# Attention over tiles of 128 neighbouring tokens, with score rows in four strips by residue

## The chip, the cores and the metric

The kernel runs on one core of one Trainium2 chip. The metric is the device time of one execution in microseconds. Before the change three runs gave a median of 2524.17 us (2521.6 to 2528.89).

## The reference

One inference step of a two-layer decoder, for a prompt of 512 tokens and 8 sample sequences of 8 tokens, 576 columns in all, model width 1024. Layer 0 mixes with a Mamba-2 SSD block, layer 1 with a dilated sliding-window attention; each is placed between two half-weighted SwiGLU feed-forward blocks. The change touches the attention of the prompt:

```
for g, (win, dil) in enumerate(((128, 1), (512, 4), (2048, 16))):     # 8 heads of 64 in each group
    idx = qi[:, None] - dil * j[None, :]            # j = 0 .. win // dil: keys by stride
    s = q . k[idx] - slope[g, h] * dil * j          # masked where idx < 0
    o[g], lse[g] = softmax(s) @ v[idx], logsumexp(s)
w = softmax(lse over the three groups);  out = sum_g w[g] * o[g]      # then @ w_o
```

Since the groups' outputs are weighted by their softmax denominators, one softmax over the keys of all three groups gives the same. For head h of each group the kernel therefore takes a single softmax over the keys of group 0 (the last 129 tokens), of group 1 (earlier tokens of the same residue modulo 4) and of group 2 (of the same residue modulo 16).

## The kernel before

The kernel runs as instruction streams written out by hand for each engine (SyncE starts DMAs, GpSimd, ScalarE, TensorE, VectorE), synchronized by counted semaphores. Each engine executes its stream in order. Activations stand feature-major, 576 tokens along the free axis.

Large products are made in three parts of split fp32 (`product`, L1441): high weights by high and by low activations, then low weights by high activations; a unit of 128 output features is 48 matmuls of 288 columns. ScalarE makes the high part of the weights (L895), GpSimd the low part (L743). ScalarE's `high_u` (L903) and VectorE's `low_u` (L2141) make the parts of the normalized input; for the attention (n == 4) both write the 512 prompt tokens permuted, residue t of 4 first, then a = token // 4, so that `qkv` holds tokens by residue. VectorE also makes a permuted copy of the reciprocal root (`rmp`, L2811).

`attention` has four turns (`turn(c, last)`), each with two heads of every group. The nine units of projections of turn 0 come first. In turns 0 to 2 the nine projection units of the next turn (`ahead(k)`) are interleaved with the attention of this one; the last turn has none. A turn has in order:

- 12 transposes of the values (L1977), copied out by ScalarE;
- for the tile t of 128 queries of residue t: `wide_scores` against all 512 keys of group 0 (L1962), one matmul a head, and `narrow_scores` against the 128 keys of the same residue in groups 1 and 2 (L1969), one a head and group;
- `softmax_in` on VectorE (L2850): three bias operations, slope times distance plus score, 512, 128 and 128 wide, a maximum over 768 and its negation; `exps` on ScalarE (L1332) with the sum; `normalize` on VectorE (L2866);
- 12 transposes of probabilities (L2021) in three groups of four, `probs_out` on ScalarE for each group (L1350, L1352);
- `values` (L2024): six blocks of 128 keys for each of two heads, L2033;
- `heads_out` (L1356) and `heads_low` (L2904), the high and low parts of the head outputs, written back in the permuted order;
- the sample's attention in steps between these (`sample_scores` L1991, `sample_step`), on a bank of its own; `sample_own` on VectorE stands ahead of `normalize(0)`;
- the output projection of the turn (L2110 to L2112), 48 matmuls.

In turns 0 to 2 the order on TensorE for a tile t is: projection, sample step, transposes group 0, wide scores of t + 1, transposes group 1, narrow scores of t + 1, transposes group 2, projection, sample step, values. In the last turn scores run two tiles ahead. An fp32 matmul stands in the trace as two records, each with a weight load, a transpose as one.

## Time and profile before

| | us |
|---|---|
| median of three runs | 2524.17 |
| the profiled execution | 2517.44 |
| its span | 2515.6 |
| TensorE busy | 2448.1 |
| VectorE busy | 1892.7 |
| ScalarE busy | 1421.6 |

The attention begins at about 1729 us of the span with the first projection; its turns begin at 1792.7, 1884.5, 1979.0 and 2073.4 us, and the last output projection starts at 2114.8. The profiled execution's own time is its span and what lies around it. TensorE's busy time counts modelled ends of pipelined matmuls, so the distance between the starts of neighbouring records says more on its pace than a record's length. "PEld" rows are its weight loads.

### The profile page before, as it was taken

The page shows a single profiled execution, that of the slowest core. Times are in us where ns is not written, and L with a number is a line of the kernel's source. Part 1 is how long each engine was busy: PE and PEld are TensorE (multiplying, and loading weights), DVE is VectorE, ACT ScalarE, POOL GpSimd, SP SyncE. Part 2 cuts the span into 40 slices and gives each one's busy share as a digit, 9 for nine tenths or more (in the row PEclk, how much of TensorE's full clock was granted, in tenths as well). Part 3 has the DMA queues.
Part 4 walks back from the last instruction along what each step waited for, and adds up shares of the span by engine and source line. Part 5 has one row for each costly group of instructions (what it writes and reads, how often), then busy time and mean ns, then how long its engine had stood idle before and what let it go on. Part 6 is the DMA issues. An engine that isn't in the chain of part 4 may idle for free.

```text
span 2515.6 us, 48796 instructions
## 1 busy us (share of the span) xinstructions
PE 2448.1 (97%) x18955; PEld 2372.2 (94%) x18955; DVE 1892.7 (75%) x3121; ACT 1421.6 (57%) x2417; POOL 742.5 (30%) x682
## 2 busy tenths in 40 slices
PE   8999999899999998999999999999999997999998
PEld 8999999799999988999999999999998996999998
DVE  8979767878888888979776978765345448987875
ACT  7757553445555556757566757554223236766663
POOL 2222233454444542222222222223322220222223
PEclk9999999899999998999999999999999999999999
DMA  7776743123333325767655777754433423777763
GB/s 204 168 163 168 168 114 101 44 95 103 103 103 103 98 77 151 169 163 168 158 131 139 169 169 161 170 128 149 145 109 123 138 91 86 163 169 166 164 156 91
DMA packets 107137, 341.92 MB, mean 136 GB/s; under 512 B 13824, under 2 KB 17536, under 8 KB 88512
## 3 DMA queue, kind: packets, MB, share of 16 engines
q1 hardware_dynamic: 53952, 242.78, 29.0%
q0 software_dynamic: 52992, 96.49, 22.8%
q8 instruction: 131, 2.15, 0.3%
q14 instruction: 62, 0.51, 0.1%
HBM read 223.44 MB, written 19.32 MB: 96 GB/s over the span
## 4 chain that ended last, share of the span: by engine, by line
PE 85%; DVE 7%; ACT 3%; issue 3%; DMA 2%; POOL 0%; DVEq 0%; SPq 0%; ACTq 0%; POOLq 0%
PE ps L1551 14%; PE ps L1557 14%; PE ps L1549 14%; PE ps L1451 7%; PE ps L1452 7%; PE ps L1457 7%; PE ps L1566 2%; PE ps L1567 2%; DMA sb_lw<-sb_rawf 2%; PE ps L1574 2%; PE ps L1866 1%; PE ps L1867 1%; PE ps L1868 1%; PE ps L1498 1%; PE ps L1490 1%
## 5 line engine op out<-in xcount | busy, mean ns | idle before, releaser
L1551 PE MATMUL ps<-sb_ual,sb_hw 128*128 128x288 f32 x2240 | 612.2, 295 | 0.0
L1549 PE MATMUL ps<-sb_uah,sb_hw 128*128 128x288 f32 x2240 | 608.1, 294 | 0.0
L760 POOL DMA_DIRECT2D sb_lw<-sb_rawf x336 | 289.8, 864 | 961.7 <-ACT sb_lw L930 939.3
L1551 PEld LDWEIGHTS ps<-sb_ual,sb_hw 128*128 128x128 f32 x2240 | 421.2, 188 | 0.0
L1549 PEld LDWEIGHTS ps<-sb_uah,sb_hw 128*128 128x128 f32 x2240 | 420.5, 188 | 0.0
L1557 PE MATMUL ps<-sb_uah,sb_lw 128*128 128x288 f32 x2240 | 384.1, 293 | 1.6 <-DMA sb_lw<-sb_rawf 1.0
L743 POOL TENSOR_TENSOR sb_wl<-sb_raw,sb_wh 128x1024 fp32r<-128x1024 f32 (+1 forms) x106 | 260.2, 2458 | 424.7 <-ACT sb_wh L895 408.7
L1451 PE MATMUL ps<-sb_uh,sb_wh 128*128 128x288 f32 x1360 | 377.4, 304 | 5.8 <-DVE sb_zs L2578 3.2
L1452 PE MATMUL ps<-sb_ul,sb_wh 128*128 128x288 f32 x1360 | 369.4, 298 | 0.0
L1557 PEld LDWEIGHTS ps<-sb_uah,sb_lw 128*128 128x128 f32 x2240 | 328.0, 188 | 3.2 <-DMA sb_lw<-sb_rawf 1.7
L1451 PEld LDWEIGHTS ps<-sb_uh,sb_wh 128*128 128x128 f32 x1360 | 258.2, 190 | 15.7 <-issue 7.0
L929 ACT CAST sb_hw<-sb_rawf 128x512 fp32r<-128x512 f32 x336 | 207.7, 618 | 92.1 <-PE ps L1557 81.6
L1452 PEld LDWEIGHTS ps<-sb_ul,sb_wh 128*128 128x128 f32 x1360 | 258.4, 190 | 0.4
L1549 PE MATMUL ps<-sb_hh,sb_hw 128*128 128x288 f32 x896 | 244.1, 294 | 3.9 <-DVE sb_x L2331 3.9
L1551 PE MATMUL ps<-sb_hl,sb_hw 128*128 128x288 f32 x896 | 243.9, 295 | 0.0
L895 ACT CAST sb_wh<-sb_raw 128x1024 fp32r<-128x1024 f32 (+1 forms) x106 | 111.5, 1052 | 182.7 <-PE ps L1457 126.4
L930 ACT ACTIVATE sb_lw<-sb_rawf 128x512 fp32r<-128x512 f32 x336 | 211.5, 629 | 0.0
L2204 DVE TENSOR_TENSOR sb_lw<-sb_tw,sb_hw 128x1024 fp32r<-128x1024 f32 x112 | 137.2, 1225 | 95.3 <-ACT sb_hw L964 90.6
L964 ACT CAST sb_hw<-sb_tw 128x1024 fp32r<-128x1024 f32 x112 | 117.8, 1052 | 136.5 <-PE ps L1557 136.5
L1457 PE MATMUL ps<-sb_uh,sb_wl 128*128 128x288 f32 x1360 | 194.1, 295 | 0.0
L1457 PEld LDWEIGHTS ps<-sb_uh,sb_wl 128*128 128x128 f32 x1360 | 185.0, 188 | 0.0
L1549 PEld LDWEIGHTS ps<-sb_hh,sb_hw 128*128 128x128 f32 x896 | 168.1, 188 | 5.7 <-issue 5.5
(346 smaller groups left out, 5197.2 us busy)
## 6 DMA issues: line engine op xcount, KB each, us to landing
sb_lw<-sb_rawf POOLq DMA_DIRECT2D x368, 256.0 KB, 3.8
sb_rawf<-w_ffn_in SPq DMA_DIRECT2D x87, 1024.0 KB, 5.3
sb_rawf<-w_ffn_so SPq DMA_DIRECT2D x32, 1024.0 KB, 5.6
sb_raw<-w_ssd SPq DMA_DIRECT2D x64, 512.0 KB, 3.6
sb_raw<-w_att SPq DMA_DIRECT2D x40, 512.0 KB, 3.6
sb_rawf<-w_ffn_out SPq DMA_DIRECT2D x32, 384.0 KB, 3.0
sb_h<-state SPq DMA_DIRECT2D x8, 1024.0 KB, 4.9
ssm_sample<-sb_h SPq DMA_DIRECT2D x8, 1024.0 KB, 4.7
```

Source lines behind the costliest of these rows:

```text
L743: pool.tensor_tensor(wl[parity][:, 0:width], raw[:, parity, 0:width], wh[parity][:, 0:width].bitcast(F32), ALU.subtract).then_inc(wl_done, 1)
L760: pool.dma_start(slot(lw, p), rawf[:, s % 2, i * BL:(i + 1) * BL], accum_op=ALU.add).then_inc(ld_in[i], 16)
L929: nc.scalar.copy(slot(hw, p), src).then_inc(hd_done, 1)
L930: nc.scalar.activation(slot(lw, p), src, ACT.Copy, scale=-1.0).then_inc(nd_done, 1)
L964: nc.scalar.copy(slot(hw, 7, 2), tw[:, 2 * BL:4 * BL]).then_inc(ht34_done, 1)
L1451: pe.matmul(ps[:, b, 0:n], w, rh[:, k, t0:t0 + n], start=first and k == 0, stop=False)
L1452: pe.matmul(ps[:, b, 0:n], w, rl[:, k, t0:t0 + n], start=False, stop=False)
L1457: ins = pe.matmul(ps[:, b, 0:n], w, rh[:, k, t0:t0 + n], start=False, stop=last and k == nk - 1)
L1549: pe.matmul(out, w[:, k * P:(k + 1) * P], high[k], start=begins and k == 0, stop=False, skip_group_check=True)
L1551: pe.matmul(out, w[:, k * P:(k + 1) * P], low[k], start=False, stop=False, skip_group_check=True)
L1557: ins = pe.matmul(out, v[:, k * P:(k + 1) * P], high[k], start=False, stop=k == 3, skip_group_check=True)
L2204: V.tensor_tensor(slot(lw, 7, 2), tw[:, 2 * BL:4 * BL], slot(hw, 7, 2).bitcast(F32), ALU.subtract).then_inc(lt34_done, 1)
```

## The change

The projections now write `qkv` in the tokens' own order. `high_u`, `low_u` and the reciprocal root lose their permuted forms. A tile t is the 128 neighbouring tokens 128 t to 128 t + 127; its score rows are arranged in four strips of 32 partitions, one for each residue q modulo 4. For each strip and head, near scores are one matmul with 32 stationary columns (the queries of residue q, 4 elements apart) against 128 (t = 0) or 256 contiguous keys of group 0; far scores, for groups 1 and 2, are one matmul against the 32 (t + 1) keys of that residue, 4 elements apart. A tile thus has 24 score matmuls in place of 6, and its keys are 192, 384, 448 or 512 wide in place of 768.

All scores of a head lie in one bank, so one bias operation covers them, with a table whose group 1 and 2 columns carry the ratio of the slopes. `pr` gets two buffers for tiles. The transposes (3 a head for t = 0, 4 otherwise, in place of 6; those of far keys are 32 (t + 1) columns wide) go back into the bank of the scores and are copied out once a head. `values` has 2 or 4 matmuls of near keys with 128 columns and 16 of far keys with 32 (t + 1) rows and 32 columns, in place of 12. The value transposes of groups 1 and 2 read their tiles 4 elements apart. On TensorE the transposes of a tile now stand together, both heads' scores follow the values two tiles ahead, and scores(0) and scores(1) stand at the head of every turn.

The diff, cut to what the prediction speaks of:

```diff
+KEYS = (192, 384, 448, 512)
...
-            pt = at("pt", [P, 2, 768])
-            pr = at("pr", [P, 2, 768])
-            d0 = at("d0", [P, CH, SEQ])
+            pt = at("pt", [P, 2, SEQ])
+            pr = at("pr", [P, 2, 2, SEQ])
+            dist = at("dist", [P, sum(KEYS)])
...
+        def of_residue(ap, r):
+            return ap.rearrange("p (b r) -> p r b", r=DIL)[:, r, :]
...
+        def by_residue(ap):
+            return ap.rearrange("p (b r) -> p r b", r=DIL)
+        def residue(ap):
+            return ap.rearrange("p (r b) -> p r b", r=DIL)
...
+        def near_keys(t):
+            return P * min(t + 1, 2)
...
+        def far_keys(t):
+            return 32 * (t + 1)
...
+        def score_bank(t, j):
+            return 4 + 2 * (t % 2) + j
...
+        def head_bank(t, last):
+            return t % 2 if last else 2
...
-                if n == 4:
-                    dst = uh[:, m, 0:SEQ].rearrange("p (t a) -> p t a", t=DIL)
-                    nc.scalar.activation(dst, perm(x[:, m, 0:SEQ]), ACT.Copy, scale=gains[:, n, one(m)])
-                    nc.scalar.activation(uh[:, m, SEQ:TOK], x[:, m, SEQ:TOK], ACT.Copy,
-                                         scale=gains[:, n, one(m)]).then_inc(uh_done, 1)
-                elif n != last_norm:
+                if n != last_norm:
                     nc.scalar.activation(uh[:, m, :], x[:, m, :], ACT.Copy, scale=gains[:, n, one(m)]).then_inc(uh_done, 1)
...
-                        nc.scalar.activation(pr[:, e % 2, :], pr[:, e % 2, :], ACT.Exp, bias=nmx[:, e:e + 1],
+                        t, j = e // 2, e % 2
+                        p = pr[:, t % 2, j, 0:KEYS[t]]
+                        nc.scalar.activation(p, p, ACT.Exp, bias=nmx[:, e:e + 1],
                                              accum_out=den[:, e:e + 1]).then_inc(exp_done, 1)
...
-                    def probs_out(t, i):
-                        act.wait_ge(pt_mm, c * 12 + (3 * t + i + 1))
-                        if t and i == 0:
+                    def probs_out(t, j):
+                        act.wait_ge(pt_mm, c * 8 + (2 * t + j + 1))
+                        if t and j == 0:
                             act.wait_ge(pv_mm, c * 4 + t)
...
+                        w = near_keys(t) + 2 * P
+                        nc.scalar.copy(pt[:, j, 0:w], ps[:, score_bank(t, j), 0:w]).then_inc(pt_done, 1)
...
                     def heads_out(t):
                         act.wait_ge(pv_mm, c * 4 + (t + 1))
-                        nc.scalar.copy(perm(oh[:, 0:SEQ])[:, t, :], ps[:, head_bank(last), 0:P]).then_inc(oh_done, 1)
+                        nc.scalar.copy(by_residue(oh[:, rows(t)]), residue(ps[:, head_bank(t, last), 0:P])).then_inc(oh_done, 1)
...
-                    def wide_scores(t):
-                        if t:
-                            pe.wait_ge(max_done, c * 8 + 2 * t)
+                    def scores(t):
+                        near, n = near_keys(t), far_keys(t)
+                        if t >= 2:
+                            pe.wait_ge(pt_done, c * 8 + (2 * (t - 2) + 2))
                         for j in range(2):
                             r = slice(HD * j, HD * j + HD)
-                            pe.matmul(ps[:, 4 + j, :], qkv[r, 0, rows(t)], qkv[r, 1, 0:SEQ], start=True, stop=True)
-                    def narrow_scores(t):
+                            for q in range(DIL):
+                                pe.matmul(ps[32 * q:32 * q + 32, score_bank(t, j), 0:near], of_residue(qkv[r, 0, rows(t)], q),
+                                          qkv[r, 1, (t + 1) * P - near:(t + 1) * P], start=True, stop=True)
                         for g in (1, 2):
-                            for j in range(2):
-                                r = slice(HD * j, HD * j + HD)
-                                ins = pe.matmul(ps[:, 6 + j, rows(g - 1)], qkv[r, 3 * g, rows(t)],
-                                                qkv[r, 3 * g + 1, rows(t)], start=True, stop=True)
+                            for q in range(DIL):
+                                for j in range(2):
+                                    r = slice(HD * j, HD * j + HD)
+                                    far = ps[32 * q:32 * q + 32, score_bank(t, j), near + (g - 1) * n:near + g * n]
+                                    keys = of_residue(qkv[r, 3 * g + 1, 0:DIL * n], q)
+                                    ins = pe.matmul(far, of_residue(qkv[r, 3 * g, rows(t)], q), keys, start=True, stop=True)
                         ins.then_inc(sc_mm, 1)
...
-                    for g in range(AG):
-                        for t in range(CH):
-                            ins = pe.transpose(ps[:, value_bank(g), rows(t)], qkv[:, 3 * g + 2, rows(t)], ident[:, :])
+                    for t in range(CH):
+                        ins = pe.transpose(ps[:, value_bank(0), rows(t)], qkv[:, 2, rows(t)], ident[:, :])
+                    ins.then_inc(vt_mm, 1)
+                    for g in (1, 2):
+                        for q in range(DIL):
+                            ins = pe.transpose(ps[:, value_bank(g), rows(q)], of_residue(qkv[:, 3 * g + 2, 0:SEQ], q), ident[:, :])
                         ins.then_inc(vt_mm, 1)
...
                     pe.wait_ge(ao_evac, c * 8 + 1)
-                    wide_scores(0)
-                    narrow_scores(0)
+                    scores(0)
+                    scores(1)
...
+                    def transposes(t, j):
+                        pe.wait_ge(norm_done, c * 8 + (2 * t + j + 1))
+                        near, n = near_keys(t), far_keys(t)
+                        for k in range(near // P):
+                            pe.transpose(ps[:, score_bank(t, j), rows(k)], pr[:, t % 2, j, rows(k)], ident[:, :])
+                        for g in (1, 2):
+                            probs = pr[:, t % 2, j, near + (g - 1) * n:near + g * n]
+                            ins = pe.transpose(ps[0:n, score_bank(t, j), rows(near // P + g - 1)], probs, ident[:, :])
+                        ins.then_inc(pt_mm, 1)
+                    def values(t):
+                        blocks, n = near_keys(t) // P, far_keys(t)
+                        pe.wait_ge(pt_done, c * 8 + (2 * t + 2))
...
+                            pe.wait_ge(ol_done, c * 4 + (t - 1 if last else t))
+                        for k in range(blocks):
                             for j in range(2):
                                 r = slice(HD * j, HD * j + HD)
-                                v = vt[:, max(0, k - 3), k if k < 4 else t, r]
-                                ins = pe.matmul(ps[r, head_bank(last), 0:P], v, pt[:, j, rows(k)], start=k == 0, stop=k == 5)
+                                pe.matmul(ps[r, head_bank(t, last), 0:P], vt[:, 0, t + 1 - blocks + k, r], pt[:, j, rows(k)],
+                                          start=k == 0, stop=False, skip_group_check=True)
+                        for g in (1, 2):
+                            for q in range(DIL):
+                                at = (blocks + g - 1) * P + 32 * q
+                                for j in range(2):
+                                    r = slice(HD * j, HD * j + HD)
+                                    ins = pe.matmul(ps[r, head_bank(t, last), 32 * q:32 * q + 32], vt[0:n, g, q, r],
+                                                    pt[0:n, j, at:at + 32], start=False, stop=g == 2, skip_group_check=True)
                         ins.then_inc(pv_mm, 1)
...
-                        wide_scores(1)
-                        narrow_scores(1)
                         for t in range(CH):
-                            for i in range(3):
-                                transposes(t, i)
+                            for j in range(2):
+                                transposes(t, j)
                             sample_step((0, 2, 4, 0)[t])
                             values(t)
                             if t < CH - 2:
-                                wide_scores(t + 2)
-                                narrow_scores(t + 2)
+                                scores(t + 2)
...
-                            transposes(t, 0)
-                            if t < CH - 1:
-                                wide_scores(t + 1)
-                            transposes(t, 1)
-                            if t < CH - 1:
-                                narrow_scores(t + 1)
-                            transposes(t, 2)
+                            for j in range(2):
+                                transposes(t, j)
                             pe.wait_ge(q_evac, c * 9 + (10 + 2 * t))
                             ahead(2 * t + 1)
                             sample_step(2 * t + 1)
                             values(t)
+                            if t < CH - 2:
+                                scores(t + 2)
...
                 g = gains[:, n, one(m)]
-                if n == 4:
-                    for v in ((lambda a: perm(a[:, m, 0:SEQ]), lambda a: a[:, m, 0:SEQ].rearrange("p (t a) -> p t a", t=DIL)),
-                              (lambda a: a[:, m, SEQ:TOK],) * 2):
-                        ins = V.scalar_tensor_tensor(v[1](ul), v[0](x), g, v[1](uh).bitcast(F32), ALU.mult, ALU.subtract)
-                    ins.then_inc(u_ready, 1)
-                else:
-                    V.scalar_tensor_tensor(ul[:, m, :], x[:, m, :], g, uh[:, m, :].bitcast(F32),
-                                           ALU.mult, ALU.subtract).then_inc(u_ready, 1)
+                V.scalar_tensor_tensor(ul[:, m, :], x[:, m, :], g, uh[:, m, :].bitcast(F32),
+                                       ALU.mult, ALU.subtract).then_inc(u_ready, 1)
...
-                dve.wait_ge(att_const, 80)
-                V.tensor_copy(rmp[:, 0:SEQ].rearrange("p (t a) -> p t a", t=DIL), perm(rms[:, 0:SEQ]))
-                step(V.tensor_copy(rmp[:, SEQ:TOK], rms[:, SEQ:TOK]))
+                dve.wait_ge(att_const, 64)
...
-                    d, src, r = two(dst), ps[:, b:b + 2, 0:HALF], two(rmp[:, :])
+                    d, src, r = two(dst), ps[:, b:b + 2, 0:HALF], two(rms[:, :])
...
-                        if t:
-                            dve.wait_ge(pt_mm, c * 12 + (3 * t - 1 + j))
-                        V.scalar_tensor_tensor(pr[:, j, 0:SEQ], d0[:, t, :], slp[:, one(c * 2 + j)], ps[:, 4 + j, :],
-                                               ALU.mult, ALU.add)
-                        for g in (1, 2):
-                            o = slice(SEQ + (g - 1) * P, SEQ + g * P)
-                            ins = V.scalar_tensor_tensor(pr[:, j, o], d12[:, g - 1, :], slp[:, one(c * 2 + (AH * g + j))],
-                                                         ps[:, 6 + j, rows(g - 1)], ALU.mult, ALU.add)
-                        step(ins)
-                        step(V.reduce_max(nmx[:, e:e + 1], pr[:, j, :], AX.X))
+                        if t >= 2:
+                            dve.wait_ge(pt_mm, c * 8 + (2 * (t - 2) + j + 1))
+                        p = pr[:, t % 2, j, 0:KEYS[t]]
+                        step(V.scalar_tensor_tensor(p, dist[:, sum(KEYS[:t]):sum(KEYS[:t + 1])], slp[:, one(c * 2 + j)],
+                                                    ps[:, score_bank(t, j), 0:KEYS[t]], ALU.mult, ALU.add))
+                        step(V.reduce_max(nmx[:, e:e + 1], p, AX.X))
...
-                        V.tensor_scalar(pr[:, e % 2, :], pr[:, e % 2, :], rcp[:, e:e + 1], None, ALU.mult).then_inc(norm_done, 1)
+                        p = pr[:, e // 2 % 2, e % 2, 0:KEYS[e // 2]]
+                        V.tensor_scalar(p, p, rcp[:, e:e + 1], None, ALU.mult).then_inc(norm_done, 1)
```

## Rows read from the trace of the kernel before

**Rows 1.** The page's busy times of the engines.

```profile
PE 2448.1 (97%) x18955; PEld 2372.2 (94%) x18955; DVE 1892.7 (75%) x3121; ACT 1421.6 (57%) x2417; POOL 742.5 (30%) x682
```

**Rows 2.** Busy time by window: start:end, length, then PE, PEld, DVE, ACT, POOL, clock, DMA.

```profile
1733.00:1792.70 59.70, 56.83 (x408) 56.03 (x408) 15.63 (x15) 10.76 (x11) 23.70 (x12) 0.97 0.51 181
1792.70:1884.50 91.80, 91.04 (x807) 83.06 (x807) 43.47 (x107) 31.90 (x58) 24.02 (x10) 1.00 0.36 123
1884.50:1979.00 94.50, 93.67 (x825) 85.50 (x825) 46.55 (x112) 30.63 (x57) 24.04 (x10) 1.00 0.35 120
1979.00:2073.40 94.40, 93.61 (x827) 85.52 (x826) 46.18 (x112) 30.62 (x57) 24.02 (x10) 1.00 0.34 115
2073.40:2116.00 42.60, 30.46 (x351) 23.41 (x350) 32.59 (x93) 20.37 (x47) 0.00 (x0) 0.96 0.20 71
```

**Rows 3.** The waits of PE, 1730 to 2150: us in total, times, longest.

```profile
PE ps L1962 <- DVE sb_nmx L2864: 5.7, 3, 2.5
```

**Rows 4.** Timeline, weight loads in bursts: start, length, instruction, count.

```profile
486.50 0.31 PEld L1749 LDWEIGHTS ps<-sb_sgs,sb_xds 64*64 64x64 f32 x8 [0.17 <-issue]
...
1795.67 0.25 PEld L2000 LDWEIGHTS ps<-sb_ident,sb_qkv 128*64 128x64 f32 x3
...
1815.83 1.29 PEld L2033 LDWEIGHTS ps<-sb_pt,sb_vt 128*64 128x64 f32 x24 [0.16 <-issue]
...
1843.38 1.69 PEld L2059 LDWEIGHTS ps<-sb_vc,sb_pts 128*32 128x32 f32 x64
...
1863.12 1.36 PEld L2021 LDWEIGHTS ps<-sb_ident,sb_pr 128*128 128x128 f32 x12
```

**Rows 5.** Timeline of tile 0 of turn 0: transposes and scores, to the next projection.

```profile
1805.81 0.49 PEld L2021 LDWEIGHTS ps<-sb_ident,sb_pr 128*128 128x128 f32 x4
...
1806.46 1.13 PE L1962 MATMUL ps<-sb_qkv 64*128 64x512 f32 x4
...
1808.11 0.72 PE L1969 MATMUL ps<-sb_qkv 64*128 64x128 f32 x8
...
1809.24 0.19 PEld L1451 LDWEIGHTS ps<-sb_uh,sb_wh 128*128 128x128 f32 x1
```

**Rows 6.** Timeline: the start of scores(0), and of the projection behind values(0).

```profile
1794.16 0.30 PEld L1962 LDWEIGHTS ps<-sb_qkv 64*128 64x128 f32 x4 [0.17 <-issue]
...
1817.29 0.19 PEld L1451 LDWEIGHTS ps<-sb_uh,sb_wh 128*128 128x128 f32 x1 [0.17 <-issue]
```

**Rows 7.** ScalarE, permuted and plain copies of the input: by line, and by form.

```profile
L907 ACT ACTIVATE sb_uh<-sb_x,sb_gains x8: 1208/1224/1237, 1699.5 to 1730.4; 128x512 fp32r<-128x512 f32 x8
...
L1008 ACT ACTIVATE sb_uah<-sb_x,sb_gains 128x576 fp32r<-128x576 f32 x8 | 6.1, 762 | 2.4 <-DVE sb_x L2947 2.4
```

**Rows 8.** Groups by form, 1780 to 2140: busy us, mean ns, idle before.

```profile
L2856 DVE SCALAR_TENSOR_TENSOR sb_pr<-sb_d,sb_slp,ps 128x512 f32<-128x512 f32 x32 | 23.9, 746 | 31.0 <-PE ps L1969 28.4 <-PE ps L2021 2.5
L2860 DVE SCALAR_TENSOR_TENSOR sb_pr<-sb_d,sb_slp,ps 128x128 f32<-128x128 f32 x64 | 19.2, 342 | 0.0
L2863 DVE TENSOR_REDUCE sb_nmx<-sb_pr 128x1 f32<-128x768 f32 x32 | 30.5, 953 | 1.1
L2868 DVE RECIPROCAL sb_rcp<-sb_den 128x1 f32<-128x1 f32 x32 | 5.1, 158 | 5.4 <-ACT sb_pr L1334 5.3
L2869 DVE TENSOR_SCALAR sb_pr<-sb_pr,sb_rcp 128x768 f32<-128x768 f32 x32 | 19.9, 621 | 1.1
L1334 ACT ACTIVATE sb_pr<-sb_pr,sb_nmx 128x768 f32<-128x768 f32 x32 | 30.0, 937 | 26.9 <-DVE sb_nmx L2864 26.9
```

**Rows 9.** Timeline of the last turn: first probability transposes, start of the output projection.

```profile
2083.05 0.66 PE L2021 MATMUL ps<-sb_ident,sb_pr 128*128 128x128 f32 x4
...
2114.79 0.37 PE L2110 MATMUL ps<-sb_oh,sb_wh 128*128 128x288 f32 x1 [0.99 <-DVE sb_ol L2904]
```

**Rows 10.** Timeline of PE ahead of and behind the first projection.

```profile
1704.99 0.41 PE L1566 MATMUL ps<-sb_hh,sb_hw 128*128 128x288 f32 x1 [0.45 <-DVE sb_x L2474]
...
1733.26 0.40 PE L1451 MATMUL ps<-sb_uh,sb_wh 128*128 128x288 f32 x1 [0.48 <-DVE sb_ul L2148]
```

76 lines of the change are left out of this document (24 added, 52 removed).

## Prediction

> **What bounds the kernel now.** I read the busy shares first: TensorE (PE) is busy 97% of the span, VectorE 75%, ScalarE 57% [rows 1]. Then the busy time by window, cut at the attention's turns. In the three turns that are mixed with projections (c = 0 to 2) PE is busy 91.04 of 91.80 us, 93.67 of 94.50 and 93.61 of 94.40; in the last turn, which has none, only 30.46 of 42.60, with VectorE at 32.59 [rows 2]. So there are two regimes. In turns 0 to 2 the time is PE's own, and a change there is worth what it does to PE's instructions. In turn 3 the chain scores, bias and maximum (VectorE), exp (ScalarE), normalize (VectorE), transpose (PE), copy (ScalarE), values (PE) sets the end. The waits of PE confirm it: of its idle time the largest entry is L1962 waiting 5.7 us for the negated maximum [rows 3].
>
> **The unit prices of PE.** I use the distance between starts of neighbouring weight loads, since matmul ends are modelled. One fp32 matmul is two records, one fp32 transpose one. Per record: a 128-column transpose 113 ns (12 of them in 1.36 us, less the last one's 0.14); a 64-column transpose 70 ns; a 64-column matmul with 128 moving columns 53 ns (24 in 1.29 us); the sample matmuls of 32 columns in alternating column strips 26 ns (64 in 1.69 us); and the nearest row to the new short matmuls, L1749 with 64 by 64 and 64 moving columns, 8 records in 0.31 us less 0.13, so 25 ns [rows 4]. A matmul with N moving columns thus costs 2N/2.4 ns a record divided by the number of array tiles that alternate (512 wide, two heads: 213 ns), with about 26 ns the least that any row shows.
>
> **Turns 0 to 2, PE, old.** The block of transposes and next scores of a tile runs from 1805.81 to 1809.24, 3.43 us, three times a turn; scores(0) 1794.16 to 1795.67, 1.51; the last transposes 1.36; values 1815.83 to 1817.29, 1.46, four times [rows 4 to 6]. Sum 10.29 + 1.51 + 1.36 + 5.84 = 19.0 us a turn.
>
> **New.** Transposes: 48 become 30: 14 of near keys at 113 ns, 16 of far keys (32 to 128 columns) at 90, between the 70 and 113 of the rows: 3.0 us. Scores: near, 16 records a tile, 27 ns at 128 keys and 53 at 256: 0.43 + 3 x 0.85 = 3.0; far, 32 records a tile at 27: 3.4. Values: near 4 then 3 x 8 records at 53 = 1.5; far 32 a tile at 27: 3.4. Each change of the array's shape leaves a gap: the old blocks hold about 0.2 each (3.43 us against 12 x 0.107 + 0.85 + 0.43 of streaming, over four changes). The new order has about 12: in and out of values (8, of half that size), near to far values where the far rows are 32 or 64 (2), around scores (6): 2.4 us. Sum 16.7, so -2.3 a turn.
>
> The value transposes stay 12 a turn, but 8 now load a tile whose columns are 4 elements apart. No PE row here shows such an operand. The nearest are on ScalarE: L907 with stride 4 takes 1224 ns for 512 elements where L1008 takes 762 for 576 at stride 1, about twice a column [rows 7]. Bounds: nothing, or 2.0 ns a column in place of 0.83, +1.2 us a turn. I take a doubled load, 8 x 107 ns = +0.86. Net -1.44 a turn, -4.3 us for three. VectorE and ScalarE get less work in these turns and both are under half busy [rows 2], so nothing of theirs surfaces: normalize(0) has a whole projection unit to be ready in, as now. The extra scores(1) at the turn's head only moves work.
>
> **The last turn.** VectorE per head and tile: 746 + 2 x 300 (the 342 ns forms overlap by some 40) + 953 + 2 x 158 (reciprocal, and the negation at the same price) + 621 = 3.23 us, times 8 = 25.8 [rows 8]. By the slopes of the same rows (bias 1.05 ns a column, maximum 1.05, normalize 0.55) the widths 192, 384, 448, 512 cost 0.41+0.35+0.31, 0.61+0.55+0.41, 0.68+0.62+0.45, 0.75+0.69+0.48; two heads and the 0.31 of small operations: 15.1 us, -10.7. Exp goes from 937 ns to 400, 580, 640, 700. Not all of that is on the path. I walked the turn from the value transposes (2073.43) with these prices: scores(1) now precede the sample's scores, and sample_own, which stands in VectorE's queue ahead of normalize(0), waits for them until about 2080.3; PE is free of the sample's scores at 2082.1; first transposes 2082.1 (2083.05 now); T(1) 2087.8; T(2) 2093.9; the sample's value step, whose L2059 burst alone is 1.69 us [rows 4], then stands between T(2) and values(2) as now, and exp(6) waits in ScalarE's queue behind heads_out(2), 2100.1; T(3) 2102.0; output projection 2106.8, against 2114.79 now [rows 9]. With the strided value transposes, 0.86 later: -7.2 us.
>
> **Ahead of the attention.** The permuted copies go: high_u from 1224 ns and a second short piece to about 762 in one [rows 7], low_u alike. PE stalls twice behind that chain, 0.45 us at 1704.99 and 0.48 at 1733.26 [rows 10]; with both engines' pieces nearly halved it runs ahead of PE, and with the restart of the array I count -1.1. In the window 1733.00 to 1792.70 the granted clock is 0.97 [rows 2]: since it has two levels, 2.4 and 1.2 GHz, 0.06 x 59.7 = 3.6 us were at the lower one, after PE's idle stretches there, which costs 1.8 us. One such stretch goes; I count a quarter of it, -0.5, with 0 and -1.8 as bounds. The permuted copy of the root lies on VectorE under a projection that PE runs anyway: nothing. Smaller tables on SyncE: nothing.
>
> Sum: -4.3 - 7.2 - 1.6 = **-13.1 us**. The profiled execution took 2517.44 us (span 2515.6), so it would take 2504.3; it lies 6.7 below the median of the three timed runs, 2524.17 (2521.6 to 2528.89), and on that footing I forecast **2511 us**.
>
> **Rivals.**
> *The far values' loads don't overlap.* They have 64 stationary columns and start at the same rows; if the loads of the two column halves go one after the other, a record costs 53 ns, not 27, as in L2033, whose 53 fits both readings. L1749's 25 ns speaks against it, though with half as many rows. Price: 32 x 0.026 = 0.85 us a tile, on the path in all 16 tiles: +13.6, so 2525, no change. The Trainium skill ("TensorE: Matmul & The Clock Gate", Part 3) says that weight loads overlap matmuls in flight only when their row group differs, which is this rival's rule. L2033's pitch does not bear the rule out, since its loads share rows and still hide.
>
> *Strided reads decide, slower.* The far scores stream keys 16 bytes apart, four column strips from the same partitions. If such an element costs ScalarE's 2.0 ns and the strips share that port, a tile of width n takes 16 x n x 2.0 ns (the two heads sit on different partitions): 1.02, 2.05, 3.07, 4.10, in all 10.2 us a turn in place of 3.4, +6.8, times four = +27; with the dearer value transposes +1.4, 2511 + 28 = 2539, slower than before. It decides from the second tile on. For it: both ScalarE and VectorE show the penalty. Against: PE streams an fp32 element at half its clock's rate, and four strips read the same partitions at full speed in the sample's matmuls. The Trainium skill ("Advanced Engine Details and Errata", Memory Cachelines) gives the rule: SBUF lines are 16 bytes and at least two hits a line are needed for full speed, and a stride of four fp32 misses that. ScalarE's rows agree; no run here shows it on PE yet.
>
> *More than forecast.* If the two heads' near scores overlap, being on different rows, near scores halve: -1.5 a turn, and T(3) could come earlier: 2504.
>
> **Chances.** Forecast 0.56 (own range 2504 to 2518), more than forecast 0.08, loads 0.19, strides 0.17. Faster and slower are counted from 0.3% (7.6 us), about what a measurement tells from no change. Faster: 0.51 + 0.08 = 0.59; the forecast's weak end 0.05, and 0.14 of the loads' case, give 0.19 for the same; slower 0.05 + 0.17 = 0.22. The range leaves the strided case out and a little below: 2500 to 2531.
>
> **What would show it.** Far score and value records 26 to 27 ns apart (53 or more: a rival). Strided value transposes at about 213 ns, not 113. The turns 0 to 2 at 90.4, 93.1 and 93.0 us; the last turn's output projection 34 us after its first value transpose, where it was 41.4. No PE wait for VectorE's uh or ul parts near 1704 and 1733. I am wrong if turns 0 to 2 grow, or if the last turn gains less than 5 us, which would mean that another wait took over the VectorE work's place.

## The result and the profile after

The changed kernel takes 2499.2 us (median of four runs, 2495.7 to 2502.22), the kernel before 2523.41 beside it: ratio 0.990, 95% interval 0.988 to 0.992. On another chip it was 2502.65 against 2525.12, ratio 0.991 (0.990 to 0.993). So 22 to 24 us faster, where 13 were forecast; 2499.2 lies just below the range given. The profiled execution took 2495.7 us, span 2493.9, 21.7 less than before.

The page's busy times, which answer to [rows 1]: 15 us less of PE, 34 of VectorE.

```profile
PE 2433.2 (98%) x19699; PEld 2369.0 (95%) x19699; DVE 1859.0 (75%) x3047; ACT 1393.9 (56%) x2393; POOL 741.5 (30%) x682
```

Busy time by window in the changed kernel, columns as in [rows 2]: from the sums of squares to the first value transpose, the turns 0 to 2, the end of the last turn, the first 10 us of its output projection.

```profile
1734.20:1789.40 55.20, 52.59 (x391) 51.80 (x389) 10.57 (x10) 9.97 (x10) 23.49 (x12) 1.00 0.51 172
1789.40:1878.90 89.50, 88.47 (x1005) 83.42 (x1006) 38.31 (x93) 26.19 (x54) 24.05 (x10) 1.00 0.39 127
1878.90:1968.50 89.60, 88.58 (x1008) 83.52 (x1007) 39.19 (x95) 24.94 (x53) 24.07 (x10) 1.00 0.38 127
1968.50:2058.00 89.50, 88.49 (x1007) 83.45 (x1006) 39.15 (x95) 24.92 (x53) 24.02 (x10) 1.00 0.36 121
2078.00:2089.30 11.30, 8.04 (x157) 6.91 (x155) 4.46 (x13) 3.85 (x12) 0.00 (x0) 0.81 0.29 94
2089.30:2099.30 10.00, 9.16 (x43) 8.46 (x44) 7.52 (x11) 7.35 (x13) 1.74 (x2) 0.71 0.24 43
```

The turns are still PE's: its idle time in each is 1.0 us. The last two rows show its clock at the lower level for part of the time just when the last values and the output projection run. Its waits from 1700 to 2150, which answer to [rows 3]: the 5.7 us behind the negated maximum are gone, and what is late now is the normalized tile, of which one wait alone is 1.5 us.

```profile
PE ps L2023 <- DVE sb_pr L2867: 2.9, 3, 1.5
PE ps L2000 <- ACT sb_vts L1351: 2.2, 4, 0.6
...
PE ps L2040 <- ACT sb_pt L1360: 1.3, 2, 0.7
...
PE ps L1459 <- DVE sb_qkv L2825: 0.8, 3, 0.3
```

Timeline of PE in turn 0: near values (L2040) and far values (L2047) of tile 0, then near scores (L1972) and far scores (L1980) of tile 2, then the next projection; below it the values of tile 1 with the scores of tile 3. They answer to [rows 5, 6]. The second block runs from 1827.97 to 1831.15, 3.2 us.

```profile
1810.61 0.44 PE L2040 MATMUL ps<-sb_pt,sb_vt 128*64 128x128 f32 x4
1810.98 1.12 PE L2047 MATMUL ps<-sb_pt,sb_vt 32*64 32x32 f32 x32
1812.03 0.69 PE L1972 MATMUL ps<-sb_qkv 64*32 64x256 f32 x16
1812.51 0.90 PE L1980 MATMUL ps<-sb_qkv 64*32 64x96 f32 x32
1813.34 0.40 PE L1459 MATMUL ps<-sb_uh,sb_wh 128*128 128x288 f32 x1
...
1827.97 0.66 PE L2040 MATMUL ps<-sb_pt,sb_vt 128*64 128x128 f32 x8
1828.56 1.12 PE L2047 MATMUL ps<-sb_pt,sb_vt 64*64 64x32 f32 x32
1829.61 0.69 PE L1972 MATMUL ps<-sb_qkv 64*32 64x256 f32 x16
1830.10 1.13 PE L1980 MATMUL ps<-sb_qkv 64*32 64x128 f32 x32
1831.15 0.40 PE L1459 MATMUL ps<-sb_uh,sb_wh 128*128 128x288 f32 x1
```

Timeline of the weight loads at the turn's head, plain (L1986) and with stride (L1990). A strided load lasts 208 ns where a plain one lasts 140, yet the eight strided ones start 119 ns apart (1.04 us for eight, less 0.208, over seven), against 111 for the plain ones of [rows 4] by the same sum (the prediction has 113).

```profile
1789.36 0.42 PEld L1986 LDWEIGHTS ps<-sb_ident,sb_qkv 128*128 128x128 f32 x4 [1.08 <-DVE sb_qkv L2825]
1789.75 1.04 PEld L1990 LDWEIGHTS ps<-sb_ident,sb_qkv 128*128 128x128 f32 x8
```

**Where the time went.** A turn is counted from one first value transpose to the next. In the kernel before these start at 1792.7, 1886.2, 1979.8 and 2073.4 us, so the first three windows of [rows 2], which are 91.8, 94.5 and 94.4 long, are not quite whole turns. All in us, each kernel in two profiled executions:

| stretch | before | before, again | after | after, again |
|---|---|---|---|---|
| sums of squares to first value transpose | 56.7 | 56.7 | 55.2 | 55.2 |
| turn 0 | 93.5 | 93.5 | 89.5 | 89.4 |
| turn 1 | 93.6 | 93.6 | 89.6 | 89.6 |
| turn 2 | 93.6 | 93.6 | 89.5 | 89.5 |
| last turn, to its output projection | 41.4 | 41.3 | 31.3 | 30.1 |
| to the last group of that projection | 9.4 | 9.4 | 10.3 | 9.4 |
| from there to the end | 391.5 | 392.7 | 394.3 | 393.8 |
| first value transpose at | 1792.7 | 1802.3 | 1789.4 | 1799.3 |

In the first pair, from unrounded times: -12.1 in turns 0 to 2, -10.0 in the last turn, -1.5 in the first row, -1.5 by two stalls that are gone ahead of it; then +0.9 and +2.9 behind, and -0.4 before any changed instruction: -21.7. The last row says why only stretches are compared below: the same kernel's first value transpose differs by 10 us between executions, with nothing of the change in it.

### The profile page after: what moved, and what is told of

Same layout as the page of the kernel before. It is cut to its first block, busy times and chain, and to the rows that moved or that the text cites. A ratio compares the mean times of both kernels' runs of the same rounds, so it can differ in the third digit from the quotient of the medians.

```text
span 2493.9 us, 50155 instructions
## 1 busy us (share of the span) xinstructions
PE 2433.2 (98%) x19699; PEld 2369.0 (95%) x19699; DVE 1859.0 (75%) x3047; ACT 1393.9 (56%) x2393; POOL 741.5 (30%) x682
## 4 chain that ended last, share of the span: by engine, by line
PE 85%; DVE 7%; ACT 3%; issue 3%; DMA 2%; POOL 0%; DVEq 0%; SPq 0%; ACTq 0%; POOLq 0%
PE ps L1559 15%; PE ps L1565 14%; PE ps L1557 14%; PE ps L1459 7%; PE ps L1460 7%; PE ps L1465 7%; DMA sb_lw<-sb_rawf 2%; PE ps L1574 2%; PE ps L1575 2%; PE ps L1582 2%; PE ps L1874 1%; PE ps L1875 1%; PE ps L1876 1%; PE ps L1506 1%; PE ps L1498 1%
## 5 line engine op out<-in xcount | busy, mean ns | idle before, releaser
L757 POOL TENSOR_TENSOR sb_wl<-sb_raw,sb_wh 128x1024 fp32r<-128x1024 f32 (+1 forms) x106 | 260.4, 2460 | 410.8 <-ACT sb_wh L909 394.3
L1459 PE MATMUL ps<-sb_uh,sb_wh 128*128 128x288 f32 x1360 | 375.6, 302 | 6.2 <-DVE sb_zs L2581 3.2
L1459 PEld LDWEIGHTS ps<-sb_uh,sb_wh 128*128 128x128 f32 x1360 | 256.6, 189 | 17.9 <-issue 7.5
```

What stands on the lines that cost most here:

```text
L757: pool.tensor_tensor(wl[parity][:, 0:width], raw[:, parity, 0:width], wh[parity][:, 0:width].bitcast(F32), ALU.subtract).then_inc(wl_done, 1)
L1459: pe.matmul(ps[:, b, 0:n], w, rh[:, k, t0:t0 + n], start=first and k == 0, stop=False)
```

## The experiments

Each starts from the changed kernel. "Turn" is the mean of turns 0 to 2 (89.5 there); "last" runs to the output projection (31.3 and 30.1), "projection" from there to its last group (10.3 and 9.4).

| | time | ratio to before, 95% | turn | last | projection |
|---|---|---|---|---|---|
| heads_apart | 2505.01 | 0.991 to 0.995 | 90.8 | 32.9 | 10.3 |
| near_mixed | 2502.22 | 0.990 to 0.994 | 89.6 | 31.9 | 10.3 |
| no_stride | 2499.21 | 0.989 to 0.992 | 88.4 | 34.4 | 10.3 |
| keys_plain (one run) | 2498.66 | | 88.8 | 31.2 | 10.3 |
| strip_by_strip | 2502.73 | 0.991 to 0.996 | 90.3 | 31.8 | 10.3 |
| front_back | 2502.65 | 0.991 to 0.995 | 89.6 | 31.3 | 10.3 |
| three_bias | 2505.53 | 0.991 to 0.995 | 89.5 | 32.7 | 10.3 |
| early_exp | 2499.03 | 0.988 to 0.992 | 89.6 | 28.2 | 9.4 |
| filler | 2501.4 | 0.989 to 0.993 | 89.5 | 30.1 | 9.4 |
| last_order | 2499.91 | 0.989 to 0.992 | 89.6 | 30.2 | 10.0 |
| last_order2 | 2498.72 | 0.989 to 0.992 | 89.6 | 27.9 | 9.4 |

The runs of one kernel on one chip lie 2 to 10 us apart; the turns repeat within 0.1. The last two columns hold the clock as well: 10.3 us in "projection" stands wherever the granted clock fell for about 10 us around the projection's start, 9.4 where it did not, and last_order's 10.0 with a shorter fall.

**Do the two heads' value records overlap?** The loops over heads and residues change places, in `values` and in the far part of `scores`; cut to the loop heads:

```diff
-                for q in range(DIL):
-                    for j in range(2):
+                for j in range(2):
+                    for q in range(DIL):
```

> The changed kernel, with the short records of the residues issued head by head (in scores() and values() the loop over the two heads lies outside the loop over the four residues), so that neighbouring value records write the same half of the PE columns. Theory A (the pitch of the short records is the time of one record divided by the number of different tiles that neighbouring records lie on): value records go from 28 ns to 53 ns, 32 of them from 1.01 to about 1.7 us, +0.7 us a tile; the score records still alternate over the four strips of one head, 53 ns over 4 is less than their 23 ns, so they stay. Turns 0 to 2 +2.8 us each (89.6 to 92.4), last turn about +2 us, together about +10 us: 2509 us. Theory B (a record costs a fixed 20 to 28 ns to issue, wherever it lies): nothing changes, 2499 us.

The turn grew by 1.2 us, 0.3 a tile: between both theories. Timeline of tile 1: from the start of the 32 far value records to the next group 1.36 us where it was 1.05, so 10 ns a record more, 38 for the 28 that the loads show; the far scores stay at 1.13.

```profile
1835.17 1.43 PE L2047 MATMUL ps<-sb_pt,sb_vt 64*64 64x32 f32 x32
1836.53 0.69 PE L1972 MATMUL ps<-sb_qkv 64*32 64x256 f32 x16
```

So the alternation of heads is worth something, but not a factor of two: theory A's size fell, and theory B with it.

**Do the near scores gain from eight tiles in a row?** Heads inside, residues outside, in the near loop.

> The changed kernel, with the near score records of the two heads alternating (loop over residues outside, heads inside): eight tiles in place of four. Theory A (pitch is stream time over the number of tiles: 107 ns over 4 is the 27 ns seen): the 16 near records of a tile with 256 keys go from 0.48 us to the 20 to 23 ns pitch of the far ones, 0.32 to 0.37 us; three such tiles a turn, -0.4 us a turn, -1.5 us in all: 2497.5 us. Theory B (27 ns is the cost of issuing a record): no change in scores(), 2499 us.

No change (89.6 us; the 16 near records 0.69 us as before). My reading of four tiles was wrong rather than the idea: a tile's near scores are eight matmuls on eight different tiles in either order. By the prediction's rule a record with 256 columns takes 2 x 256/2.4 = 213 ns on its tile, and over eight tiles 27 ns, which is near the pitch seen (1829.61 to 1830.10, 16 records, 31 ns with what lies between).

**Does the stride cost?** The same sizes, read contiguously, so the kernel computes with other tokens; no_stride does it for queries, far keys and value transposes, keys_plain for the far keys alone.

```diff
-    keys = of_residue(qkv[r, 3 * g + 1, 0:DIL * n], q)
+    keys = qkv[r, 3 * g + 1, q * n:(q + 1) * n]
```

> The changed kernel reads contiguous tokens where it read every fourth one (queries and far keys of scores(), values of the value transposes), so its scores and values are of other tokens; sizes and counts are the same. Theory A (a stride of 16 bytes does not slow a record's pitch on PE): scores() keep their 0.58, 1.1, 1.3 and 1.5 us, the value transposes go from 1.55 to 1.45 us, turns 89.5 us, 2499 us. Theory B (the rest of the prediction's term: the strided load is slower, 208 ns against 140, and holds the stream up): the strided reads still cost, turns get shorter by 0.5 to 1 us each, 2496 us.

> The changed kernel in which only the far keys of scores() (the moving operand) are read contiguously, so scores are of other tokens; queries and value transposes keep their stride. Theory A (the stride costs only on the operand that streams): turns 0 to 2 take 88.5 to 88.6 us, nearly all of no_stride's 1.1 us; the 32 far records with 128 keys go from 1.13 to about 0.7 us. Theory B (it is the strided weight load, 137 ns in place of 106, that costs): 89.4 us and 1.1 us as in the changed kernel.

It does. Turns went to 88.4 us with no_stride (-1.1), to 88.8 with keys_plain (-0.7). Timeline of tile 3's scores in no_stride: the far group with 128 keys lasts 0.69 us where the changed kernel has 1.13.

```profile
1834.39 0.66 PE L1972 MATMUL ps<-sb_qkv 64*32 64x256 f32 x16
1834.84 0.69 PE L1980 MATMUL ps<-sb_qkv 64*32 64x128 f32 x32
1835.47 0.40 PE L1459 MATMUL ps<-sb_uh,sb_wh 128*128 128x288 f32 x1
```

Groups by form in turns 0 to 2, all three tiles of a width together (busy us, mean ns), in the changed kernel and in keys_plain:

```profile
L1980 PE MATMUL ps<-sb_qkv 64*32 64x128 f32 x96 | 3.4, 401 | 0.0
L1980 PE MATMUL ps<-sb_qkv 64*32 64x96 f32 x96 | 2.7, 346 | 0.0
L1980 PE MATMUL ps<-sb_qkv 64*32 64x64 f32 x96 | 2.3, 292 | 0.0
L1980 PE MATMUL ps<-sb_qkv 64*32 64x32 f32 x96 | 1.8, 235 | 0.0
```

```profile
L1980 PE MATMUL ps<-sb_qkv 64*32 64x128 f32 x96 | 2.2, 278 | 0.0
L1980 PE MATMUL ps<-sb_qkv 64*32 64x96 f32 x96 | 2.0, 254 | 0.0
L1980 PE MATMUL ps<-sb_qkv 64*32 64x64 f32 x96 | 2.0, 229 | 0.0
L1980 PE MATMUL ps<-sb_qkv 64*32 64x32 f32 x96 | 1.8, 216 | 0.0
```

With plain keys the width hardly matters: here is a floor. The strided keys take no longer at 32, little longer at 64 (2.3 us for 2.0) and clearly longer at 96 and 128. With 128 keys, from the far group's start to the next product is 1.05 us strided (1830.10 to 1831.15) and 0.63 plain in no_stride (1834.84 to 1835.47). Less the 0.2 us that the prediction counted for a change of shape, that is 27 and 13 ns a record, and 2 x 128/2.4 over eight tiles is 13 ns: by this estimate the stride doubles the time of the streamed operand. With nothing taken off, the ratio is 1.7. Strided queries (weights) and strided value transposes together make up the other 0.4 us a turn. The Trainium skill ("Advanced Engine Details and Errata", Memory Cachelines) says that SBUF lines are 16 bytes and that accesses that each open a new line pay; on PE's streamed operand this trace agrees, by the 1.05 us against 0.63 with 128 keys.

**Do records on one strip wait for each other?**

```diff
-    for g in (1, 2):
-        for q in range(DIL):
+    for q in range(DIL):
+        for g in (1, 2):
```

> The changed kernel with the far score records issued strip by strip (loop over residues outside, distances and heads inside): eight records in a row on one strip of 32 columns, the two heads' row halves alternating in it. Theory A (records overlap only when they lie on different strips; four strips give the 27 ns of 256 keys, and 128 keys at a stride take as long as 256 without): each record then takes its whole stream alone, twice its columns over 2.4 GHz: 0.85, 1.7, 2.6 and 3.4 us for the far records of tiles 0 to 3 where the changed kernel takes 0.56, 0.76, 0.90 and 1.13, +5 us a turn, 94.7 us, about +18 us in all, 2517 us. Theory B (the two halves of the rows overlap as well): half of that, 4.3 us in place of 3.4, +1 us a turn, 2503 us.

The turn grew by 0.8 us, near theory B's 1, but the tiles do not follow it: the 96 far records of a width are busy for 3.2, 3.4 and 4.1 us with 64, 96 and 128 keys, where B gives 2.6, 3.8 and 5.1 (three times its half). So B's total came out by luck of two errors, and theory A's size fell. Timeline, 128 keys: 1.39 us for 1.13.

```profile
1834.50 1.39 PE L1980 MATMUL ps<-sb_qkv 64*32 64x128 f32 x32
```

All scores of a turn take 5.4 us in place of 4.6, which is the whole +0.8. Eight records in a row on one strip cost far less than eight streams one after the other, so PE probably has the next strip's records under way meanwhile; what limits that was not found. The order costs 0.26 us on a tile of 128 keys, where theory A had 2.3.

**What ahead of the attention was worth 3 us?** u and its low part in two strided pieces, and the root's copy by residue into a scratch tile, put back:

```diff
+    V.tensor_copy(sqx[:, 0:SEQ].rearrange("p (t a) -> p t a", t=DIL), by_residue(rms[:, 0:SEQ]))
+    step(V.tensor_copy(sqx[:, SEQ:TOK], rms[:, SEQ:TOK]))
```

> The changed kernel with the strided copies ahead of attention put back (rms copied by residue to a scratch tile, u and its low part written in two strided pieces each), nothing else. Theory A (those copies alone made the two stalls of 0.7 us near 1704 and 1733 and the fall of the granted clock to 0.97 behind them): the first value transpose comes 3.0 us later (1792.4 in place of 1789.4), half by stalls and half by the clock, 2502 us. Theory B (the stalls come back but not the fall of the clock, which had another cause): 1.5 us later, 2500.5 us, the window from 1733 to the first value transpose at clock 1.00.

Neither theory: the 3.0 us of theory A, at the clock of theory B. The stalls are back (1.5 us), and so are the 56.7 us from the sums of squares to the first value transpose, where the changed kernel has 55.2, but at clock 1.00 (window from 1739.3):

```profile
1739.30:1796.00 56.70, 52.89 (x390) 51.86 (x388) 14.66 (x12) 9.95 (x10) 23.70 (x12) 1.00 0.48 162
```

The waits of PE from 1700 to 1800 in this kernel name the cause: a product that waits 1.2 us for the first evacuation of PSUM.

```profile
PE ps L1464 <- DVE sb_qkv L2837: 1.2, 1, 1.2
PE ps L1464 <- DVE sb_ul L2161: 0.6, 1, 0.6
PE ps L1579 <- DVE sb_x L2487: 0.5, 1, 0.5
```

The kernel before in a second record settles it.

> The kernel before, a second record. Theory A (93.5 us for each of turns 0 to 2, 41.4 us for the last, and the copies of rms ahead of the first evacuation are this kernel's; all else is the execution's): 93.5, 93.5, 93.5 and 41.4 us again, 56.7 us from the sums of squares to the first value transpose, with or without the fall of the granted clock; the place of the first value transpose differs by up to 8 us from 1792.7. Theory B (56.7 us comes from the clock's fall): without a fall, 55.2 us.

Again 56.7 us, this time without a fall of the clock. Its window, its waits, and the timeline of VectorE: the two copies of the root (L2811, L2812) hold VectorE for 4.2 us ahead of the first evacuation (L2824).

```profile
1745.60:1802.30 56.70, 52.88 (x391) 51.84 (x389) 14.65 (x12) 9.96 (x10) 23.68 (x12) 1.00 0.49 171
```

```profile
PE ps L1451 <- ACT sb_wh L895: 1.8, 1, 1.8
PE ps L1451 <- DVE sb_qkv L2824: 1.2, 1, 1.2
```

```profile
1747.55 3.75 DVE L2161 RECIPROCAL sb_rms<-sb_rms 128x576 f32<-128x576 f32 x1 [4.08 <-ACT sb_rms L900]
1751.34 1.87 DVE L2811 COPY sb_sqx<-sb_rms 128x512 f32<-128x512 f32 x1
1753.13 2.38 DVE L2812 COPY sb_sqx<-sb_rms 128x64 f32<-128x64 f32 x1
1755.55 1.42 DVE L2824 TENSOR_TENSOR sb_qkv<-ps,sb_sqx 128x576 f32<-128x576 f32 x2
```

In the first record PE ran part of those 4.2 us at the lower level, so it arrived late and no wait was to be seen: the clock's loss lay under VectorE's copy, and the copy's wait under the clock. Its windows, from the kernel before:

```profile
1739.00:1742.00 3.00, 3.00 (x17) 3.00 (x18) 2.96 (x2) 1.06 (x1) 3.00 (x3) 0.71 0.13 49
1742.00:1745.00 3.00, 3.00 (x19) 3.00 (x18) 3.00 (x2) 0.00 (x0) 3.00 (x4) 0.72 0.89 272
```

front_back puts all the copies back together; that the root's copy is 1.2 of the 1.5 us is read from the wait, not from a run with that copy alone.

**Is the single bias operation behind the turns?** Three additions in place of one, widths unchanged.

> The changed kernel with the bias of a tile and head added in three VectorE operations (near keys, far keys of each distance) in place of one, widths unchanged. From the changed kernel's own rows (0.41 us for 192 columns, 0.74 us for 512) an operation has about 0.2 us beside its columns, 0.1 of it under its neighbour. Theory A (in turns 0 to 2 TensorE sets the time, only the last turn is a chain over VectorE): turns 0 to 2 stay at 89.5 us, last turn +0.2 to 0.4 us for each of some four to six heads on the chain, +1 to +2 us: 2500.5 us. Theory B (the single operation is behind the gain of the turns): turns 0 to 2 longer by more than 0.3 us each.

Theory A. Turns 89.5, last turn 32.7, +1.4. The three of tile 3 take 0.99 us where the one takes 0.74.

**The end of the last turn.** In ScalarE's order the exponentials of tile 3 stand behind the output of tile 2. early_exp puts them ahead (its diff, cut, follows), filler gives TensorE work that nobody reads, and after_again is the changed kernel once more.

```diff
     probs_out(t, j)
+    if t == CH - 2:
+        exps(6)
+        exps(7)
     sample_step((1, 2, 4, 6)[t])
     heads_out(t)
```

> The changed kernel; in the last turn ScalarE takes the two exponentials of tile 3 ahead of the output of tile 2 and of the sample step, behind which they stood (the first began at 2081.88 in the changed kernel, its maximum was ready at 2078.5). Theory A (the end of the last turn is set by the order on ScalarE, and the fall of the granted clock by TensorE's pauses there): transposes of tile 3 start about 1.7 us earlier, the output projection about 2 us earlier (last turn 29.3 us in place of 31.3), 2497 us; if the shorter pauses also keep the clock up, up to 3 us more. Theory B (TensorE's own work of the sample step and of values(2) sets the time): last turn unchanged, 2499 us.

> The changed kernel; in the last turn TensorE does 9, 12, 5 and 8 transposes of a tile that nobody reads (113 ns each) where it waited: behind scores(2), behind the sample's last transpose, ahead of values(3) and ahead of the output projection. Theory A (the change took TensorE work out of the last turn, and its pauses bring the clock to its lower level just when values(3) and the output projection start, where it costs time): with the pauses filled the clock stays at 1.00 from 2057 to 2100, values(3) take 1.7 us in place of 2.8 and the first 10 us of the output projection and what follows 3 us less, about -3.5 us: 2495.5 us. Theory B (the clock falls there for another reason): clock falls as before, and the filling costs 0 to 1 us: 2499.5 us.

> The changed kernel itself once more, on the same chip as the two that follow. Theory A (the stretch ahead of attention differs from execution to execution whatever the kernel: 1789.4 us in the changed kernel's first record, 1791.8 to 1798.0 in those of the experiments, none of which touches it apart from front_back): the first value transpose lands anywhere in 1789 to 1798, while turns 0 to 2 are 89.5 us each and the output projection 31.3 us after the last turn's start, to 0.1 us, and the time is 2499 to 2500 us. Theory B (the experiments' builds are slower ahead of attention): 1789 to 1790 again.

early_exp and filler both ran at clock 1.00 throughout, and so did after_again, the changed kernel itself, with 30.1 and 9.4 us. Its windows at the end of the last turn and the start of the output projection, beside the 0.81 and 0.71 of the first record:

```profile
2088.00:2097.90 9.90, 6.66 (x155) 5.60 (x154) 4.34 (x13) 3.80 (x11) 0.00 (x0) 1.00 0.32 108
2097.90:2107.90 10.00, 8.00 (x50) 6.83 (x51) 8.54 (x12) 8.14 (x14) 1.87 (x3) 1.00 0.31 54
```

So the first record's fall, 1.2 us in the last turn and 0.9 in the projection, comes in some executions and not in others, and filler has not shown anything: its 30.1 is after_again's. Over all records, the order of the changed kernel's last turn has this fall in eight of nine (all but after_again; "projection" 10.3 in the table), and early_exp, filler and last_order2 have it in none of four. Fewer pauses of TensorE may therefore make it rarer, but four records do not show that. At like clock early_exp is worth 1.9 us. In the changed kernel the first of the two exponentials stood behind ScalarE's output of tile 2 (first timeline), in early_exp it starts as soon as its maximum is there (second):

```profile
2081.70 0.39 ACT L1364 CAST sb_oh<-ps 128x128 fp32r<-128x128 f32 x1 [1.21 <-PE ps L2047]
2081.88 0.71 ACT L1345 ACTIVATE sb_pr<-sb_pr,sb_nmx 128x512 f32<-128x512 f32 x1
```

```profile
2087.08 0.72 ACT L1345 ACTIVATE sb_pr<-sb_pr,sb_nmx 128x512 f32<-128x512 f32 x1 [0.56 <-DVE sb_nmx L2865]
```

**A new order for the last turn.** VectorE takes the softmax of tile 1 ahead of the sample's maximum, PE spreads the four sample steps over tiles 1 to 3.

> The changed kernel with the last turn in another order: VectorE does the softmax of tile 1 ahead of the sample's maximum, ScalarE takes exponentials as soon as their maximum is there, TensorE does the four sample steps behind scores(3), ahead of and behind values(2), and behind the transposes of tile 3. Theory A (the last turn is a chain in which ScalarE's and VectorE's orders hold up work that is ready, and its pauses cost clock): last turn 28 us in place of 31.3, and the clock at its higher level for longer: 2493 to 2496 us. Theory B (TensorE's work sets the last turn): within 0.5 us of 31.3, 2499 us.

30.2 us, clock included, and not 28: I had put the sample's exponential on ScalarE ahead of the evictions of tile 1. PE stood idle for 2.45 us, and the window with that pause and the 5 us behind it, 2075.1 to 2085.1, shows 0.84; that of the projection's start, 2095.1 to 2105.1, shows 0.83.

```profile
2080.07 0.66 PE L2047 MATMUL ps<-sb_pt,sb_vt 128*64 128x128 f32 x8 [2.45 <-ACT sb_pt L1360]
```

> As last_order, but ScalarE takes the sample's exponential behind the evictions of tile 1, not ahead of them, where in last_order it held them up from 2077.2 to 2078.9 while TensorE stood idle for 2.45 us and its clock fell. Theory A (the last turn is a chain of orders, and pauses cost clock): values(1) start about 1.5 us earlier than in last_order, the output projection begins 27 to 28.5 us after the turn's first transpose (31.3 changed kernel, 28.2 early_exp, 30.2 last_order), the clock stays at 1.00 and the last output projection record starts 9.4 us later, as in early_exp. Theory B (TensorE's work is now the bound): no earlier than early_exp, 28.2 us.

27.9 us, and 9.4 behind: 0.3 better than early_exp. Beside the changed kernel on one chip, four runs against five:

> last_order2 beside the changed kernel on one chip. Theory A (its last turn, 27.9 us for 31.3 to the output projection and 37.25 for 41.6 to its last record, is worth what it shows): 4.4 us faster than after_again. Theory B (what the last turn gives is taken back in the network that follows, whose weights then come later): within 1.5 us of it.

2497.35 us against 2502.65; ratios to before 0.988 to 0.991 and 0.990 to 0.993. The stretches say 2.2 us against after_again (27.9 and 30.1, the rest alike) and 4.3 against the changed kernel's first record, which has the clock's fall (37.3 and 41.6 with the projection); the medians' 5.3 cannot tell these apart, since only one run of each was profiled. It is the best version here, by a little.

## Why the prediction was wrong

The direction and the two regimes came out, and the rivals that foresaw no gain or a loss were refuted. The sizes of all three terms failed: turns 0 to 2 by -7.8 us, the last turn by -2.8, the part ahead by -1.4; +3.4 us in stretches for which nothing was forecast hides some of that.

**Turns 0 to 2: -1.44 a turn forecast, -4.0 measured.** The step that failed is the price of the scores: the near ones at 53 ns with 256 keys, as if spread over four tiles, the far ones at 27 ns, "about 26 ns the least that any row shows", used as a floor. The blocks of turn 0, each from its first record's start to that of what follows, in us:

| | before | forecast, gaps included | after |
|---|---|---|---|
| transposes of probabilities | 5.86 | 3.0 | 3.81 |
| scores | 6.92 | 7.6 | 4.61 |
| values | 5.84 | 6.1 | 6.04 |
| sum | 18.62 | 16.7 | 14.46 |
| value transposes | 1.46 | 2.32 | 1.54 |

All scores of a turn take 0.58, 1.17, 1.31 and 1.54 us for tiles 0 to 3: near 1.7 where 3.0 were forecast, far 2.9 where 3.4 were, with the 1.2 us of gaps that the forecast counted beside them inside these figures. The rule 2N/2.4 over the tiles in use was sound for scores, with eight tiles and a doubling for the stride: 20 and 27 ns for 96 and 128 far keys, as measured (0.83 and 1.05 us, less 0.2, over 32). So 27 ns was right for tile 3 by luck, a stream of 13 ns doubled by the stride, and too dear for the others. The least that plain keys show lies at about half of 26 ns. The rows read as a floor were streams: 2 x 64/2.4 over two column halves is 27 ns for L1749, and 2 x 128/2.4 over four strips is 27 ns for the sample's matmuls [rows 4].

Values hit: 28 ns a record for 27. But here the rule without a floor would have given 13 ns (2 x 32/2.4 over two column halves), so something other than streamed columns sets 28; heads_apart's 38, with neighbours on the same column half, shows that the neighbour matters, and no run separates the causes. Transposes of far keys cost 109 ns from start to start, not 90.

14.46 - 18.62 is -4.16, with 0.08 more for the value transposes and 0.1 for all else that PE does: the -4.0 measured. A wait of 0.3 us a turn for an evacuation (L1459), which the kernel before has not, lies in that 0.1; what is shorter against it was not looked for.

**Value transposes: +0.86 forecast, +0.1 measured.** The strided load is longer (208 ns for 140) but lies beside the stream before it.

**The last turn: -7.2 forecast, -10.0 (or -11.2 at full clock).** The walk had the first transposes 8.7 us into the turn and they came after 7.1, T(1) 12.6 for 14.4, T(2) 18.3 for 20.5, T(3) 25.5 for 28.6. So 1.6 of the 3.1 us were there before the first transposes, where the scores and value transposes stand that were priced too dear; the walk does not say what it charged between the later steps, and which of those was too dear stays open. From T(3) to the output projection it took 5.8 us in the first record and 4.6 in after_again, for 4.8 and the late transposes' 0.86. The bottleneck that it named, exp(6) behind heads_out(2), was the real one: early_exp got 1.9 us from it. The VectorE prices were right: 0.41, 0.60, 0.68 and 0.74 us for the bias where 0.41, 0.61, 0.68 and 0.75 were forecast.

**Ahead of the attention: -1.6 forecast, -3.0 measured.** The stalls gave 1.5 for 1.1. The clock's term was a wrong cause: before has 56.7 us with the fall and without. And "the permuted copy of the root lies on VectorE under a projection that PE runs anyway: nothing" is the step that failed: 4.2 us of it stood ahead of the first evacuation, for which the third product waits 1.2 us.

**The rivals.** Loads that don't overlap: not so, the 32 far value loads take 1.01 us, 28 ns each. The Trainium skill ("TensorE: Matmul & The Clock Gate", Part 3) has weight loads overlap matmuls in flight only where the row group differs; these share their rows, so this trace does not agree. Strides decide: the mechanism is real and the size was not. The rival priced tile 3's far scores at 4.10 us by ScalarE's 2.0 ns a column, and they take 1.13; plain keys would save 0.7 us a turn, not 6.8. "More than forecast", which had the two heads' near scores overlap and save 1.5 us a turn, was the case that came, and had 0.08: near scores took 1.7 us for 3.0.

**What was given back** is not settled in full: behind the output projection the first pair shows +2.9 us and the second +1.1. All other records of changed kernels have 392.7 to 395.3 there, the two of before 391.5 and 392.7, so 1 to 2 us may be real. A wait for a DMA of low parts does not explain it: the changed kernel's first record has one of 0.3 us there and before's second record one of 1.2, the two others none. No experiment touched this stretch.

## What to carry to other kernels

The shortest pitch seen in a trace is no floor until several widths stop at it: work out first what that row had to stream, as stream time over tiles in use, and ask what each new loop has of both. Take the floor from a loop of the same shape: here scores went down to 13 ns and values stayed at 28. A copy on an engine that is busy only part of the time can still be late, if the first release of a buffer stands behind it; and a slow clock can hide such a wait, so the same stretch is best read in two executions.

## What the runs showed of the hardware

- fp32 matmuls of 64 rows by 32 columns on eight tiles: with 128 streamed columns, a group of 32 records takes 0.63 us with plain columns and 1.05 with columns 16 bytes apart, an estimated 13 and 27 ns a record once 0.2 us for the change of shape is taken off. With plain columns 32 to 128 cost nearly the same (1.8 to 2.2 us for 96 records).
- Eight such records in a row on one strip cost 0.26 us more a tile of 128 keys (1.39 for 1.13), no multiple.
- A weight load with a stride of 16 bytes lasts 208 ns for 140, yet eight start 119 ns apart: nearly hidden.
- Value records with 32 streamed columns and 64 stationary ones keep 28 to 30 ns whether 32, 64, 96 or 128 rows are used, 38 to 40 with heads not alternating.
- The granted clock's fall at the end of the attention differs between executions of one kernel: 1.00 in one record, 0.71 over 10 us in another, worth 2.1 us. In no_stride it fell already behind the last turn's start, to 0.57 over 10 us from 2070.0, and that last turn took 34.4 us.
